# Two-layer block with gated linear recurrences: other PSUM banks for the turned state, level zero ahead of the state product, and the last modulation tile behind level eight

## The reference, cut to what matters

```python
mod_x = (cond_x @ w_mod[l] + b_mod[l])[:, None, :]      # six vectors of 1024 per layer
mod_c = (cond_c @ w_mod[l] + b_mod[l])[None, None, :]
...
def hgrn2_mix(q, iv, zf, zb, g, lbf, lbb, s0f, s0b):
    logf_f, k_f = forget_terms(zf, lbf)
    o_f, s_f = gla_chunk(q, k_f, iv, logf_f, s0f)
    logf_b, k_b = forget_terms(zb, lbb)
    o_b, s_b = gla_chunk(flip(q), flip(k_b), flip(iv), flip(logf_b), s0b)
    ...
def step(s, xs):                                        # inside gla_chunk
    qc, kc, vc, dc = xs
    o = jnp.einsum('bchk,bhkv->bchv', qc, s)
    s = dc[..., None] * s + jnp.einsum('bchk,bchv->bhkv', kc, vc)
    return s, o
```

## Time and profile before

| | |
|---|---|
| median of 3 runs | 4057.24 us (4054.39 to 4061.6) |
| the profiled execution | 4046.82 us, its span 4045.0 us |
| busy share of the span | PE 81%, DVE 61%, POOL 41%, ACT 34% |
| mean granted PE clock | 0.929 of full |
| stage A | 226.49 to 275.26 us, 48.77 us |
| stage B | 275.26 to 338.33 us, 63.07 us |
| stage C | 2104.26 to 2161.42 us, 57.16 us |

### The profile page before, as it was taken

One profiled execution on the slowest core, in us unless ns is written; L12 is line 12 of the kernel. 1 busy time (PEld: TensorE's weight loads), 2 busy tenths in 40 slices (PEclk: granted clock), 3 DMA queues, 4 the chain that ended last, 5 costly groups with the idle time before them and its releaser, 6 DMA issues. The chain is left out here.

```text
span 4045.0 us, 42202 instructions
## 1 busy us (share of the span) xinstructions
PE 3271.7 (81%) x13636; PEld 2079.7 (51%) x13636; DVE 2453.7 (61%) x5321; ACT 1372.9 (34%) x2942; POOL 1675.2 (41%) x1761
## 2 busy tenths in 40 slices
PE   6977986777777776677887777676779999999999
PEld 4845732223223332222576522232248978888788
DVE  4365746656556566665365755565557667676575
ACT  3364311112111111111365211111135566555664
POOL 0020566666666666666131566666630030000300
PEclk8989998888888888899998898898889999999999
DMA  5253699999999999999344899999964525455254
GB/s 194 104 220 124 228 365 354 371 364 363 368 359 361 372 361 365 353 365 378 135 157 167 325 376 353 377 358 364 372 247 176 207 84 188 177 181 202 84 188 146
DMA packets 247946, 1095.56 MB, mean 271 GB/s; under 512 B 28337, under 2 KB 31793, under 8 KB 228529
## 3 DMA queue, kind: packets, MB, share of 16 engines
q0 software_dynamic: 221184, 805.40, 51.8%
q1 hardware_dynamic: 26544, 287.47, 19.5%
HBM read 1091.72 MB, written 1.05 MB: 270 GB/s over the span
## 5 line engine op out<-in xcount | busy, mean ns | idle before, releaser
L2087 PE MATMUL ps<-v_rows,diagonal 128*128 128x512 f32 x3072 | 1542.4, 655 | 593.1 <-issue 271.0
L2087 PEld LDWEIGHTS ps<-v_rows,diagonal 128*128 128x128 f32 x3072 | 617.5, 209 | 1496.6 <-issue 1230.2
L1960 DVE CUSTOM_DVE_ANT_0 u_rows<-u_rows,ps 128x1024 f32<-128x1024 f32 x768 | 921.8, 1220 | 676.9 <-DMA u_rows<-in_u,experts 394.7
L1932 POOL DMA_INDIRECT v_rows<-in_v,experts x768 | 728.7, 949 | 482.0 <-issue 215.1
L1922 POOL DMA_INDIRECT u_rows<-in_u,experts x768 | 734.5, 956 | 341.9 <-issue 234.5
L2006 ACT ACTIVATE hidden<-hidden 128x2 f32<-128x2 f32 x384 | 77.5, 203 | 1716.0 <-DVEq L1962 865.7
L2842 PE MATMUL ps<-h_high_low,weights_high 128*128 128x512 f32 x1408 | 499.5, 400 | 6.5 <-DVE h_high_low L2697 6.3
L3265 DVE TENSOR_TENSOR weights_low<-ring,weights_high 128x1024 fp32r<-128x1024 f32 (+1 forms) x328 | 402.9, 1240 | 2.7 <-ACT weights_high L3258 2.5
L2843 PE MATMUL ps<-h_high_low,weights_low 128*128 128x256 f32 x1408 | 395.2, 281 | 0.0
L3258 ACT ACTIVATE weights_high<-ring 128x1024 fp32r<-128x1024 f32 (+1 forms) x328 | 338.7, 1033 | 99.7 <-PE ps L2843 54.1
L2842 PEld LDWEIGHTS ps<-h_high_low,weights_high 128*128 128x128 f32 x1408 | 265.4, 188 | 74.0 <-DVE h_high_low L2697 6.2
(11 more groups left out here) (357 smaller groups left out, 4029.1 us busy)
## 6 DMA issues: line engine op xcount, KB each, us to landing
ring<-in_ffn_gu SPq DMA_DIRECT2D x44, 2048.0 KB, 8.3
ring<-in_w_in SPq DMA_DIRECT2D x26, 2048.0 KB, 8.2
ring<-in_w_mod SPq DMA_DIRECT2D x24, 2048.0 KB, 9.5
ring<-in_ffn_down SPq DMA_DIRECT2D x32, 1408.0 KB, 6.0
ring<-in_peer_wq SPq DMA_DIRECT2D x8, 2048.0 KB, 8.6
u_rows<-in_u,experts POOLq DMA_INDIRECT x768
v_rows<-in_v,experts POOLq DMA_INDIRECT x768
ring<-in_w_out SPq DMA_DIRECT2D x4, 2048.0 KB, 10.2
```

Source lines behind the costliest of these rows:

```text
L1932: pool.indirect_dma_start(self.VROWS[n % self.v_slots][:, :], None, m.dram["v"], bass.IndirectOffsetOnAxis(ap=self.IDX[:, n:n + 1], axis=0 ...
L1960: dve.tensor_tensor_reduce(rows[:, :], rows[:, :], self.rows(), 1.0, 0.0, ALU.mult, ALU.add, self.HID[:, t % 2, s + r:s + r + 1])
L2087: mm = pe.matmul(self.A.ps[:, self.Y_BANK + half, :], self.DIAG[:, (g % DIAGONALS) * GROUP + r, :], rows[:, half * 512:(half + 1) * 512], ...
```

## The change

The change touches the three recurrence stages and nothing else.

- The turned blocks go to banks 1, 2, 3 and 7, the state's products to banks 1 and 3.
- On PE level zero and level one stand ahead of the state's product; on ACT `first_scalar` stands ahead of the copies to `key_rows`, and the copy of the state stands behind level 2's scaling.
- The modulation tiles move to other levels: the second from ahead of level zero to behind it, the third to sixth one level or one tile later, and the seventh behind level eight.
- The turn of the modulation row stands behind the final products on PE, and the row's copy behind `att_off` on ACT; the turn's bank is 5, not 2.

```diff
-MOD_LEVELS = (-1, -1, 1, 3, 4, 6, 7)
+MOD_LEVELS = (-1, 0, 2, 4, 5, 7, 8)
...
 class FinalState:
+    TURN_BANKS = (1, 2, 3, 7)
+    STATE_BANKS = (1, 3)
...
-    def tensor(self, pe):
+    def tensor_rows(self, pe):
...                                        # the 16 transposes, now into TURN_BANKS
         mm.then_inc(m.e_turned.sem, 1)
+
+    def tensor_state(self, pe):
+        m, A = self.m, self.A
         pe.wait_ge(m.e_kept.sem, self.kept + 1)
...                                        # the 16 products, now into STATE_BANKS
+    def rows_turned(self, act):
+        act.wait_ge(self.m.e_turned.sem, self.turned + 1)
+
     def scalar_rows(self, act):
         m, A = self.m, self.A
-        act.wait_ge(m.e_turned.sem, self.turned + 1)
...
         @block.scalar
         def _(act):
             if final is not None:
-                final.scalar_rows(act)
+                final.rows_turned(act)
             tree.first_scalar(act)
             act.drain().then_inc(m.act_a.sem, 1)
             if final is not None:
-                final.scalar_state(act)
+                final.scalar_rows(act)
             act.activation(G, G, ACT.Silu)
...
                 act.drain().then_inc(m.act_a.sem, 1)
-                if level == LEVELS:
-                    beside.scalar(act)
+                if final is not None and level == 2:
+                    final.scalar_state(act)
...
             act.drain().then_inc(m.act_c.sem, 1)
+            beside.scalar(act)
             act.wait_ge(m.pe_b.sem, m.pe_b.at(1))
...
         @block.tensor
         def _(pe):
             if final is not None:
-                final.tensor(pe)
+                final.tensor_rows(pe)
...
-                if final is not None and level == 1:
-                    final.ready(pe)
...
                 mm.then_inc(m.pe_a.sem, 1)
+                if final is not None and level == 1:
+                    final.tensor_state(pe)
                 beside.products_at(pe, level)
-            beside.turn(pe)
             pe.wait_ge(m.act_c.sem, m.act_c.at(1))
             if STATE is not None:
+                final.ready(pe)
...
             mm.then_inc(m.pe_b.sem, 1)
+            beside.turn(pe)
...
-                        beside = Modulation(m, A, BESIDE_MOD[layer][s], inner, bank=0, spot=2)
+                        beside = Modulation(m, A, BESIDE_MOD[layer][s], inner, bank=0, spot=5)
```

More of the change, by code:

```diff
@@ L1185, in tensor @@
                 n = 2 * dh + half
-                mm = pe.transpose(A.ps[:, 4 + n // 4, (n % 4) * P:(n % 4 + 1) * P], self.E[:, dh, half * P:(half + 1) * P],
+                mm = pe.transpose(A.ps[:, self.TURN_BANKS[n // 4], (n % 4) * P:(n % 4 + 1) * P], self.E[:, dh, half * P:(half + 1) * P],
                                   A.const[:, C_IDENT:C_IDENT + P])
         mm.then_inc(m.e_turned.sem, 1)
+    def tensor_state(self, pe):
+        m, A = self.m, self.A
         pe.wait_ge(m.e_kept.sem, self.kept + 1)
@@ L1192, in tensor @@
             for half in range(2):
-                mm = pe.matmul(A.ps[:, 6 + dh // 4, (dh % 4) * P:(dh % 4 + 1) * P], self.KR[:, 2 * dh + half, :],
+                mm = pe.matmul(A.ps[:, self.STATE_BANKS[dh // 4], (dh % 4) * P:(dh % 4 + 1) * P], self.KR[:, 2 * dh + half, :],
                                self.IV[:, 2 * self.s + half, h * P:(h + 1) * P], start=(half == 0), stop=(half == 1))
         mm.then_inc(m.state_made.sem, 1)
+    def rows_turned(self, act):
+        act.wait_ge(self.m.e_turned.sem, self.turned + 1)
     def scalar_rows(self, act):
         m, A = self.m, self.A
-        act.wait_ge(m.e_turned.sem, self.turned + 1)
         for b in range(4):
-            act.activation(self.KR[:, 4 * b:4 * b + 4, :], A.ps[:, 4 + b, :].rearrange("p (n c) -> p n c", n=4), ACT.Copy)
+            act.activation(self.KR[:, 4 * b:4 * b + 4, :], A.ps[:, self.TURN_BANKS[b], :].rearrange("p (n c) -> p n c", n=4), ACT.Copy)
         act.drain().then_inc(m.e_kept.sem, 1)
@@ L1207, in scalar_state @@
         for b in range(2):
-            act.activation(self.STATE[:, 4 * b:4 * b + 4, :], A.ps[:, 6 + b, :].rearrange("p (n c) -> p n c", n=4), ACT.Copy)
+            act.activation(self.STATE[:, 4 * b:4 * b + 4, :], A.ps[:, self.STATE_BANKS[b], :].rearrange("p (n c) -> p n c", n=4), ACT.Copy)
         act.drain().then_inc(m.state_kept.sem, 1)
```

## The result

The changed kernel took 4034.46 us (median of five runs, 4030.92 to 4037.14), the kernel before 4057.24 in the five runs beside it (4049.08 to 4064.48): 22.8 us less, ratio 0.9944 [0.9932, 0.9956]. The forecast was 4033 in 4021 to 4048. Timed again on another chip in the end: 4044.29 against 4068.22, ratio 0.9940 [0.9924, 0.9955].

What follows compares the result with a forecast made beforehand. The three stages were taken as chains of waits, set by level 1's start and late final products. Their gains sum to 26 us, net 24 after loads and clock; median 4057.2 less 24 gives 4033, range 4021 to 4048.

Steps and rivals of the forecast that it cites:

- Heads: Starts of B and C: level 1 on DVE at 6.6 to 6.8 us, 14.9 in B before; C's level 2 waits about 1.3.
- Middles: Level 3 to the last turn: 18.4 us in A; last turns at 34.7, 34.8 and 36.1 in A, B, C.
- without PE's lateness: Middle of A: PE's late waits (0.46 and 0.77 against 0.29) taken off, so 18.85 becomes 18.4 us.
- Ends: Last turn to final products: 3.95 us in A and B, 3.7 in C, against 8.19, 9.23 and 4.41 before.
- the term for loads and clock: Late tile loads and PE's lower clock near stage ends: 0.8, 0.8 and 0.5 us lost in A, B, C.
- Tails: Final products to next stage: 6.1, 10.1 and 9.65 us in A, B, C; added tail 0.8 to 1.3 per stage.
- Sum: Three stages at 44.7, 48.9 and 49.5 us: 26 us less together, net 24 after loads and clock.
- the last loads become the bound: Rival, A and B: fifth and seventh tile share a slot, B 57.2, A 53.2; gain 9 us, 4048; chance 0.06.
- The state's product in front of level 2: Rival, B and C on PE: half clock makes level 2 3.5 us late for level 3; gain 17, 4040; chance 0.09.
- the low clock: Rival, all stages: scattered work keeps PE at 1.2 GHz; 43 us slower, 4100; chance 0.02.
- That no end moves: Rival: ACT takes PE's place ahead of level 1 and tails eat the rest; within 0.2%; chance 0.03.

Runs made afterwards that it cites:

- the head: Kernel before with only the new banks and start order of the stages; tile levels, row's copy and turn as before: 3782.1 against 3803.67 us, ratio 0.9949.
- the end: Kernel before with only the new tile levels, row's copy, turn and its bank; state's product still ahead of level zero: 3785.7 us, ratio 0.9952.
- the experiment: Kernel before with each w_mod load cut to half its columns (1 MB), every engine's work the same: 3784.01 us.
- fillers: Changed kernel with transposes of a constant, read by nothing, in PE's idle (24 behind level 1 in A, 8 behind level 3, 12 ahead of sixth tile): 3778.1 us.
- The two other profiles: Changed kernel run again without edits, beside the experiments and on another chip in the end: 3779.76 us; 4044.29 against 4068.22 us.
- halved loads: Changed kernel with each w_mod load cut to half its columns (1 MB), PE reading the first half twice: 3766.34 us.
- the last version: Changed kernel with fourth tile behind level 3, Silu behind the row's copy, constant transposes in PE's idle: 4036.06 us, ratio 0.9927.

## Why the prediction was right

**Heads: right, by the mechanism named.** Level 1 was to start at 6.6 to 6.8 and starts at 6.6. Level 2 in C was to wait for ACT by about 1.3: 1.45. The state's product was bounded by 3.7 and 5.47 and took 3.84. B's and C's level 3 stand at 16.4 and 17.4. The table load was priced at its row of 1.28 with Silu 0.01 behind it, against the 1.4 more of the Trainium skill's "ScalarE: Activation LUTs", section "What ACT_TABLE_LOAD costs". After, it is 1.28 and 0.01 again (2107.09, 2108.38), and C came out at 49.4 where the row's price gave 49.5.

**The two parts share their gain.** The experiments add what the sum did not ask: 16.1 for the head and 12.3 for the end, 28.4 for 21.8. Of the 6.6 shared, B has 3.5 (2.0 for the tile ahead of level zero, 1.6 for the state's product at the upper clock), C 4.1 (2.0 for the tile, 1.1 for finals at +3.7 behind the later head and +4.8 with both parts, the rest in small shifts), and A minus 0.9, which its scatter covers. The prediction took them in one piece and did not count twice.

**Middles: right, in A sized too long.** The last turns were put at 34.7, 34.8 and 36.1 and came 1.6, 1.0 and 1.0 earlier. Only A's is sure: in three profiles it stands at 33.1 to 33.5, while B's stands at 33.8, 34.7 and 34.8 and C's at 35.1, 36.1 and 35.1, so in B and C some profiles come out as forecast. From level 3 on A takes 17.1, where 18.4 was "without PE's lateness". I had taken off the waits alone. When PE is late, POOL and DVE are released together and scale side by side: 1.21 and 1.87 on DVE and 1.63 on POOL in the experiment, against 1.15, 1.42 and 1.22 where POOL was ahead by 0.7. The earlier trace rows had it too: 1.30 and 1.20 at the two late levels. In the changed kernel A's level 3 is 1.07. The Trainium skill, "SBUF — State Buffer", section "Who interferes with whom", says that a DVE instruction with two inputs in SBUF contends with a GpSimd one that reads there. By that rule, the trace agrees: both are such forms and both are longer when they start together. In B and C the same happens at level six when the fourth tile runs at the lower clock throughout. Where it took 3.64, from level 3 to the last turn took 18.4 to 18.6, as forecast; where it took 2.74 to 3.62, 17.4 to 17.7; and behind fillers, at 1.92, 17.3 and 17.4.

**Ends: the mis-sized step is the term for loads and clock.** "I take 0.8, 0.8 and 0.5" for late tiles; the finals stand at +7.3, +7.7 and +4.8 against 3.95, 3.95 and 3.7, thus 3.4, 3.8 and 1.1 late. A was at the bound of 3.5 that I had given, and B 0.3 over it. The two other profiles have 2.4 and 2.1 in A, 4.1 and 4.0 in B, 0.8 and 1.2 in C. The working followed the fifth and the seventh tile through one slot and asked if the seventh comes late; it had no wait in the profile of the result and 0.73 us in A in the two others. The late one is the sixth: its slot comes free with the fourth, which the change had put a level later, and it stands in front of level eight. The row for its time from issue to use was there, the 9.6 us of the earlier trace rows: in A the fourth tile ends at 22.5, and 22.5 + 0.2 + 9.6 = 32.3 (32.65 measured), with level seven's products over at 30.6. To this came the lower clock after the gap (3.39 and 3.50 for 1.93; in A in this profile alone of the three). Two interventions show it: the fourth tile a level earlier takes 2.9 us off the finals in B and 1.1 in C, and halved loads 3.5 and 1.1. In A halved loads take 1.8 of the 3.4 (0.5 to 0.8 of what the two other profiles have), and the lower clock ahead of level eight is the other part (1.5). The prediction also set 6.8 us beside the 9.6. The Trainium skill, "DMA: Bandwidth & Descriptors", section "Anatomy of one DMA", states that fit for transfers that GpSimd issues. These loads are SP's, so the difference does not show the fit wrong.

**Tails: right.** 6.0, 9.9 and 9.5 for 6.1, 10.1 and 9.65. That each stage's tail grows by 0.8 to 1.3 was wrong for C, where it fell from 10.3: before, C's first final products had run at the lower clock, 0.79 against 0.49.

**Sum.** 143.1 was forecast for the stages without the load term and 147.2 measured: 8.2 us of late ends, less 3.6 of earlier last turns and 0.4 of tails. The two other profiles measured 148.3 and 147.8. The term allowed 2.1, so the gain was 21.8 and not 24. That the number came so close to 4033 is in part these two errors against each other, and so in part luck.

**The rivals.** The first (the last loads become the bound) was right on the mechanism and wrong on tile and size: 7 us of late ends in A and B, with neither stage longer than before. The state's product in front of level 2 did not occur: PE's idle ahead of level 2 is 0.41 and ends by ACT. Nor did the low clock: the stages have 0.89, 0.93 and 0.97, where the earlier trace rows had 0.86, 0.86 and 0.91 (0.90 to 0.97 in the two other profiles). That no end moves was wrong by the 21.8 us.

**Open.** Why A did not gain from the earlier fourth tile was read (the seventh tile's load, 1.65) but no run took that wait away by itself. Whether the 22.8 and 23.9 of the timed runs are 21.8 and scatter, or hold a little more, the intervals (17.9 to 27.6 for the first) don't tell.

## What to carry to other kernels

When work is put off on an engine that also frees the slots of a ring, follow every slot: the load that comes late is the one whose slot the moved piece frees, two pieces on, and not the piece that was moved to the end. Price a wait not by its idle alone; the engines that it releases together may slow each other, and the engine that waited may come back at a lower clock. Where two waits follow each other, taking one away may show nothing; try both. And read a stage from more than one profile before explaining 1 us of it.

## What the runs showed of the hardware that was not expected

- DVE and POOL scaling side by side from SBUF: 3.08 us for DVE's two groups of a level and 1.63 for POOL's, against 2.57 and 1.22 with POOL 0.7 ahead (the kernel before with halved loads). Both slow in part; neither stands still.
- Where a tile of 2 MB was waited for, PE worked on it 8.4 to 9.9 us after its issue (8.4 in C, 8.75 in B, 9.9 in A) with the next load under way. With loads of 1 MB PE waited for none ahead of level eight.
- Idle of about 2 us on PE put a tile of 1.93 us at 3.4 to 3.6 in some profiles and left it at 1.93 in others of the same kernel (sixth tile in A: 3.39, 1.93, 1.92); with fillers in the gaps of the last version B and C showed a granted clock of 1.00, the upper level of 2.4 GHz, throughout.
- The stages were as long on a chip on which the kernel before took 3802 us as on one with 4068. The difference lies in the expert layers: between B and C the changed kernel took 1601 us at 355 GB/s of DMA and a granted clock of 0.97 on the one, 1777 us at 320 GB/s and 0.91 on the other. Which of the two is the cause no run shows.
